# A depthwise convolution on VectorE that takes turns with GpSimd's weight splits

## The reference, cut to what matters

```python
hx = modulate(rmsnorm(x, g_mix), sh1, sc1)
px = hx @ w_in                                  # columns: q, k, v, o, gates, then 2 x 1024 for the convolution
u = p[..., :1024] * sigmoid(p[..., 1024:])      # GLU, then per row of 64 tokens:
y = conv(u, conv_w, width 31, centred, per channel) + conv_b
y = silu(layernorm(y, cn_g, cn_b))
x = x + ga1 * (concat([mlstm(px), y]) @ w_out)
x = x + ga2 * peer(...);  return rmsnorm(x, g_final)
```

## Time and profile before

| | |
|---|---|
| median of 3 runs | 3813.11 us (3805.47 to 3814.7) |
| the profiled execution | 3817.3 us, its span 3814.6 us |
| PE busy | 3521.6 us, 92% of the span |
| POOL busy | 2081.3 us, 55% |
| DVE busy | 2068.7 us, 54% |
| ACT busy | 1104.2 us, 29% |
| mean granted clock of TensorE | 0.96 of full speed |

### The profile page before, as it was taken

How to read it: one execution, slowest core, us unless ns; L and a number is a source line. 1 busy time by engine, 2 the same in 40 slices (tenths; PEclk the granted TensorE clock), 3 DMA queues, 4 the chain that set the end, 5 groups by cost and what they waited for, 6 DMA issues and landing times.

```text
span 3814.6 us, 46495 instructions
## 1 busy us (share of the span) xinstructions
PE 3521.6 (92%) x17646; PEld 3010.7 (79%) x17646; DVE 2068.7 (54%) x3619; ACT 1104.2 (29%) x1240; POOL 2081.3 (55%) x940
## 2 busy tenths in 40 slices
PE   5776679999879979999999999999999999999997
PEld 2554457887457768999999999999888888888885
DVE  1335720010361228699367677765366666667669
ACT  3211112112332222323333344333233232233232
POOL 0255653221133354567666655666677777777773
PEclk8798889999989989999999999999999999999998
DMA  9542345222863232477767766777798888888882
GB/s 343 202 144 88 118 145 179 72 77 67 310 226 122 99 113 94 166 273 272 278 249 283 281 252 260 284 285 298 299 367 314 314 308 315 314 315 310 312 316 110
DMA packets 291478, 874.82 MB, mean 229 GB/s; under 512 B 17361, under 2 KB 78081, under 8 KB 237216
## 3 DMA queue, kind: packets, MB, share of 16 engines
q1 hardware_dynamic: 226224, 519.08, 38.7%
q0 software_dynamic: 38704, 281.20, 18.1%
q10 hardware_dynamic: 26432, 73.02, 5.0%
HBM read 803.82 MB, written 69.37 MB: 229 GB/s over the span
## 4 chain that ended last, share of the span: by engine, by line
PE 81%; DVE 6%; DMA 5%; POOL 5%; ACT 2%; issue 1%; ACTq 0%; DVEq 0%; SPq 0%
PE bank L1733 73%; POOL ring_lo L434 4%; PE bank L2012 2%; PE bank L1926 2%; DMA ring<-in_w_in 2%; DMA neurons<-tiny 2%; PE bank L1741 2%; DMA ring<-in_w_mod 1%; PE bank L1905 1%; DVE low L1322 1%; ACT w_hi L427 1%; DVE acc L1621 0%; PE bank L1995 0%; ACTq L718 0%; DVE b L1510 0%
## 5 line engine op out<-in xcount | busy, mean ns | idle before, releaser
L676 POOL TENSOR_TENSOR split<-ring,split 128x1024 fp32r<-128x1024 f32 x544 | 1304.5, 2409 | 693.5 <-ACT split L996 692.5
L1733 PE MATMUL bank<-h_hi,split 128*128 128x384 f32 (+1 forms) x4608 | 1222.1, 342 | 6.6 <-POOL split L676 5.0
L1733 PE MATMUL bank<-split,a_split 128*128 128x512 f32 x4608 | 1052.3, 391 | 17.1 <-DVE acc L1614 8.8
L996 ACT ACTIVATE split<-ring 128x1024 fp32r<-128x1024 f32 x544 | 577.2, 1062 | 1598.1 <-PE bank L1733 1569.2
L1733 PEld LDWEIGHTS bank<-split,a_split 128*128 128x128 f32 x4608 | 867.6, 188 | 201.6 <-DVE acc L1614 6.3
L1733 PEld LDWEIGHTS bank<-h_hi,split 128*128 128x128 f32 x4608 | 838.6, 188 | 27.7 <-POOL split L676 6.0
L1733 PE MATMUL bank<-h_lo,split 128*128 128x384 f32 (+1 forms) x2304 | 784.8, 341 | 0.0
L434 POOL TENSOR_TENSOR ring_lo<-ring,w_hi 128x2048 fp32r<-128x2048 f32 x47 | 330.3, 7031 | 454.9 <-ACT w_hi L427 454.9
L1733 PEld LDWEIGHTS bank<-h_lo,split 128*128 128x128 f32 x2304 | 433.4, 188 | 9.9
L1733 PE MATMUL bank<-hT_hi,w_hi 128*128 128x512 f32 (+1 forms) x768 | 296.6, 386 | 132.7 <-POOL ring_lo L434 124.9
L1614 DVE TENSOR_TENSOR acc<-acc,bank 128x512 f32<-128x512 f32 x360 | 244.6, 683 | 299.9 <-PE bank L1733 287.2
(11 more groups left out here) (265 smaller groups left out, 3624.4 us busy)
## 6 DMA issues: line engine op xcount, KB each, us to landing
ring<-in_u_emb SPq DMA_DIRECT2D x128, 1024.0 KB
ring<-in_v_emb SPq DMA_DIRECT2D x128, 1024.0 KB
ring<-in_w_mod SPq DMA_DIRECT2D x96, 1024.0 KB
ring<-in_w_in SPq DMA_DIRECT2D x48, 1024.0 KB
neurons<-tiny ACTq DMA_DIRECT2D x128, 192.0 KB
gate_table<-b ACTq DMA_DIRECT2D x6, 4096.0 KB, 14.7
weigh<-neurons SPq DMA_DIRECT2D x32, 768.0 KB
weigh<-gate_table SPq DMA_DIRECT2D x32, 768.0 KB
```

The source lines that it names most:

```text
L676: nc.gpsimd.tensor_tensor(split[:, r % 2, 1, at].bitcast(F32R), ring[:, r % 4, :, :].rearrange("p k n -> p (k n)")[:, at], split[:, r % 2, ...
L996: nc.scalar.activation(split[:, q % 2, 0, at].bitcast(F32R), ring[:, q, :, :].rearrange("p k n -> p (k n)")[:, at], ACT.Copy)\
L1733: last = mm(out_, left[a].bitcast(F32R), right[b].bitcast(F32R), start=start and n == 0, stop=stop and n == 2)
```

## The change

VectorE's 248 convolution instructions are written out without loops, and before every ninth of them (for the first 198), later before every fourteenth, VectorE waits for one more weight split: for the steps n = 0, 9, 18, ... it waits for `wsplit_made` = 10 + n/9, that is until the split of tile r = 9, 10, 11, ... is done, and from n = 198 on for r = 31, 32, 33, 34. The work per step is the same.

The padded buffer is filled by pairs of channel tiles. Behind r = 9 GpSimd makes the first four products as before, but waits for its own two products before it reports each pair. Behind r = 17 it makes the other four: two into the half of `u_pad` that the first 62 steps have freed, two into `convT` tiles 6 and 7, which nothing uses yet. Behind r = 24 it copies those two into `u_pad` with two `tensor_copy` instructions. ScalarE now waits for the products (`glu_used`) where it refills `glu`; the store of o uses the buffer of q (`spill_q`), and ScalarE's wait for the whole convolution moves from block 6 to the emptying of the first k block. Three semaphores of the last stage (`x2_back`, `ga2_loaded`, `g_final_loaded`) become one.

```diff
@@ -206,7 +206,6 @@
         u_pad = top[:, 0:4 * UPW].rearrange("p (c r w) -> p c r w", r=ROWS, w=PADW)
         row_buf_b = top[:, 3072:4096].rearrange("p (b n) -> p b n", b=2)
         spill = top[:, 0:3072]
-        spill_o = spill[:, 0:2048].rearrange("p (m t) -> p m t", t=T)
         spill_q = top[:, 8216:10264].rearrange("p (m t) -> p m t", t=T)
         spill_k = spill.rearrange("p (m t) -> p m t", t=L)
         spill_v = spill.rearrange("p (s n) -> p s n", n=NB)
@@ -324,6 +323,7 @@
         set_free = sem("set_free")
         upad_clear = sem("upad_clear")
         glu_done = sem("glu_done")
+        glu_used = sem("glu_used")
         conv_step = sem("conv_step")
         pass_full = sem("pass_full")
         ln_sub = sem("ln_sub")
@@ -399,10 +399,8 @@
         a_split_made = sem("a_split_made")
         sum_free = sem("sum_free")
         sum_full = sem("sum_full")
-        x2_back = sem("x2_back")
-        ga2_loaded = sem("ga2_loaded")
+        last_rows = sem("last_rows")
         x2s_loaded = sem("x2s_loaded")
-        g_final_loaded = sem("g_final_loaded")
         merge_step = sem("merge_step")
         merged = sem("merged")
         s_step = sem("s_step")
@@ -607,22 +605,40 @@
                     pool.wait_ge(whi_made, 1)
                 nc.gpsimd.tensor_tensor(ring_lo[:, 0, at].bitcast(F32R), ring[:, 0, kk, :], weight_slot(0)[:, at],
                                         op=ALU.subtract).then_inc(first_split if kk < QT - 1 else wsplit_made, 1)
+            def glu_product(half, c, dst):
+                nc.gpsimd.tensor_tensor(out=dst, in0=glu[:, 0, c, :].rearrange("p (r w) -> p r w", w=GRID_W),
+                                        in1=glu[:, 1, c, :].rearrange("p (r w) -> p r w", w=GRID_W),
+                                        op=ALU.mult).then_inc(glu_used, 1)
             for r in range(1, WO_R):
                 split_lo(pool, r)
-                if r in (4 * 2 + 1, 4 * 4 + 1):
-
-                    half = (r - 9) // 8
-                    pool.wait_ge(set_free, 2 + 2 * half + 2)
+                if r == 9:
+                    pool.wait_ge(set_free, 4)
                     pool.wait_ge(upad_clear, 1)
-                    if half:
-                        pool.wait_ge(conv_step, 4 * TAPS)
-                    for cc in range(4):
-                        last = nc.gpsimd.tensor_tensor(
-                            out=u_pad[:, cc, :, TAPS // 2:TAPS // 2 + GRID_W],
-                            in0=glu[:, 0, cc, :].rearrange("p (r w) -> p r w", w=GRID_W),
-                            in1=glu[:, 1, cc, :].rearrange("p (r w) -> p r w", w=GRID_W), op=ALU.mult)
-                        if cc % 2:
-                            last.then_inc(glu_done, 1)
+                    for c in range(4):
+                        glu_product(0, c, u_pad[:, c, :, TAPS // 2:TAPS // 2 + GRID_W])
+                        if c % 2:
+                            pool.wait_ge(glu_used, c + 1)
+                            pool.sem_inc(glu_done, 1)
+                if r == 17:
+                    pool.wait_ge(set_free, 6)
+                    pool.wait_ge(conv_step, 2 * TAPS)
+                    for c in range(4):
+                        glu_product(1, c, u_pad[:, c, :, TAPS // 2:TAPS // 2 + GRID_W] if c < 2 else
+                                    convT[:, 4 + c, :].rearrange("p (r w) -> p r w", w=GRID_W))
+                    pool.wait_ge(glu_used, 6)
+                    pool.sem_inc(glu_done, 1)
+                if r == 24:
+                    pool.wait_ge(conv_step, 4 * TAPS)
+                    pool.wait_ge(glu_used, 8)
+                    for c in (2, 3):
+                        last = nc.gpsimd.tensor_copy(u_pad[:, c, :, TAPS // 2:TAPS // 2 + GRID_W],
+                                                     convT[:, 4 + c, :].rearrange("p (r w) -> p r w", w=GRID_W))
+                        last.then_inc(glu_used, 1)
+                    pool.wait_ge(glu_used, 10)
+                    pool.sem_inc(glu_done, 1)
             for h in range(HEADS):
                 pool.wait_ge(s_copied, 6 * (h + 1))
@@ -795,16 +811,14 @@
                 src = bank[:, s:s + 4, :]
                 if j < 4:
                     if j == 2:
-                        act.wait_ge(glu_done, 2)
+                        act.wait_ge(glu_used, 4)
                     nc.scalar.activation(glu[:, j % 2, :, :], src, ACT.Sigmoid if j % 2 else ACT.Copy)\
                         .then_inc(set_free, 1)
                     return
                 if j == 4:
-                    act.wait_ge(glu_done, 4)
-                if j == 6:
-                    act.wait_ge(conv_step, 8 * TAPS)
+                    act.wait_ge(glu_used, 8)
                 spilled(j - 4)
-                buf = spill_q if j < 6 else spill_o
+                buf = spill_q
                 if j < 6:
                     nc.scalar.activation(buf, src, ACT.Copy, scale=HD ** -0.5).then_inc(set_free, 1)
                 else:
@@ -829,6 +843,8 @@
             def empty_kv(n):
                 spilled(4 + n)
+                if n == 0:
+                    act.wait_ge(conv_step, 8 * TAPS)
                 for b in BANK_ORDER:
                     if n >= 2:
                         dst, src = spill_v[:, b, :], bank[:, b, :]
@@ -1126,7 +1142,7 @@
                 if k == 0:
                     store_neurons(NK - 1, 1)
                     for j in range(JD):
-                        act.dma_start(x2_dense[:, j, :], x2_dram[j * P:(j + 1) * P, :]).then_inc(x2_back, 16)
+                        act.dma_start(x2_dense[:, j, :], x2_dram[j * P:(j + 1) * P, :]).then_inc(last_rows, 16)
                 if k == 3:
                     act.wait_ge(rows_used, SLOTS)
                     nc.scalar.activation(nval, nval, ACT.Gelu).then_inc(nval_gelu, 1)
@@ -1134,10 +1150,10 @@
                     act.wait_ge(act_made, 1)
                     for b in range(2):
                         act.wait_ge(neuron_stored[b], 16 * (NK // 2))
-                    act.dma_start(g_final_row, g_final[:].partition_broadcast(P)).then_inc(g_final_loaded, 16)
+                    act.dma_start(g_final_row, g_final[:].partition_broadcast(P)).then_inc(last_rows, 16)
                     for i in range(LT):
                         act.dma_start(ga2_part[i], mod_dram[3 * D + i * NB:3 * D + (i + 1) * NB].partition_broadcast(P))\
-                           .then_inc(ga2_loaded, 16)
+                           .then_inc(last_rows, 16)
             with act.Fori(1, GROUPS // 2 - 1) as i:
                 for k in range(8):
                     sweep_unit(i * 8 + k, k % 4)
@@ -1235,24 +1251,29 @@
             rest1(KT - 1)
-            for half in range(2):
-                with dve.Fori(0, 2) as i:
-                    dve.wait_ge(glu_done, i + (2 * half + 1))
-                    for tap in range(TAPS):
-                        for cc in range(2):
-                            n = 2 * tap + cc
-                            y = top[:, bass.ds(i * (2 * T) + (4120 + (4 * half + cc) * T), T)]\
-                                .rearrange("p (r w) -> p r w", w=GRID_W)
-                            u = top[:, bass.ds(i * (2 * UPW) + cc * UPW, UPW)]\
-                                .rearrange("p (r w) -> p r w", w=PADW)[:, :, tap:tap + GRID_W]
-                            w = conv_col[:, bass.ds(i * (2 * TAPS) + (4 * half + cc) * TAPS + tap, 1)]
-                            if tap == 0:
-                                nc.vector.tensor_scalar(y, u, w, chan_col[:, bass.ds(i * 2 + 16 + 4 * half + cc, 1)],
-                                                        ALU.mult, ALU.add).then_inc(conv_step, 1)
-                            else:
-                                dve.wait_ge(conv_step, i * (2 * TAPS) + (4 * TAPS * half + n - 1))
-                                nc.vector.scalar_tensor_tensor(y, u, w, y, ALU.mult, ALU.add)\
-                                    .then_inc(conv_step, 1)
+            def conv_turn(n):
+                if n < 198 and n % 9 == 0:
+                    dve.wait_ge(wsplit_made, 10 + n // 9)
+                if n >= 198 and (n - 198) % 14 == 0:
+                    dve.wait_ge(wsplit_made, 32 + (n - 198) // 14)
+            for pair in range(CTILES // 2):
+                dve.wait_ge(glu_done, pair + 1)
+                for tap in range(TAPS):
+                    for cc in range(2):
+                        n = 2 * TAPS * pair + 2 * tap + cc
+                        f = 2 * pair + cc
+                        conv_turn(n)
+                        y = convT[:, f, :].rearrange("p (r w) -> p r w", w=GRID_W)
+                        u = u_pad[:, f % 4, :, tap:tap + GRID_W]
+                        w = conv_col[:, f * TAPS + tap:f * TAPS + tap + 1]
+                        if tap == 0:
+                            nc.vector.tensor_scalar(y, u, w, chan_col[:, 16 + f:17 + f], ALU.mult, ALU.add)\
+                                .then_inc(conv_step, 1)
+                        else:
```

(7 more changed lines are left out.)

## The result

| | before | after |
|---|---|---|
| median | 3813.32 us (4 runs, 3805.47 to 3814.7) | 3692.68 us (4 runs, 3692.18 to 3693.22) |
| profiled execution, its span | 3817.3, 3814.6 us | 3693.22, 3691.2 us |

The ratio is 0.9686 (95% interval 0.9674 to 0.9698). The medians differ by 120.6 us; 113.8 were forecast, and the time of 3692.68 lies inside the range of 3690 to 3713, near its lower end.

What follows compares the result with a forecast made beforehand. TensorE was taken to stall on GpSimd's weight splits, kept out by VectorE's tap runs. A loss of 117.0 us less 1.0, 1.1, 0.9 and 0.2 gave 113.8 off 3813.1: 3699.3 us, range 3690 to 3713.

Steps and rivals of the forecast that it cites:

- What bounded: TensorE waits 114.4 us for GpSimd's weight splits, which runs of back-to-back convolution taps on VectorE keep out whole.
- The loss: Blocks with taps against blocks without, two taking 157.3 against 98.8 us: 117.0 us lost in all.
- The delays: Late splits still expected after the change: 1.0 us from nine-tap groups, 1.1 and 0.9 from buffer refills, 0.2 later.
- the split of r = 18: After GpSimd's second four products, this weight split was expected at +37.4, wanted at +35.2; 1.1 us would stay.
- the two copies: GpSimd's copies into the padded buffer, 1.3 us each, making the split of r = 25 0.9 us late.
- The first k block: A 14-tap group of 9.4 us delays the split of r = 32; cost 0 to 0.7 us, taken as 0.2.
- The sum: Whole execution: 117.0 us less four delays leaves 113.8 us off the front, 3699.3 us from the median.
- Small delays: Rival: semaphore and lock handovers of 1 us each cost 12 to 24 us over six blocks, 3711 to 3723; chance 0.11.
- The ring: Rival: splits and tap groups alternate at 10.7 us, binding from 12.35; slower (3838 us) 0.02, part of its cost (3755) 0.04.
- The signs I named: Splits at most 6 us longer, tap groups about 6 us, TensorE's wait under 15, clock near 1.00, 30 us spare.

## Why the prediction was right, point by point

- *What bounded.* Right. Splits kept out by runs of taps, and nothing else: without the turns the time is back at 3814.3.
- *The loss, 117.0 us.* The runs say 118.7: 413.3 us for six blocks less 6 x 49.1. I had taken a block from the start of one split to that of another whose second, r = 32, belongs to the k block and comes 0.6 us late; measured from place 7 to place 7 two blocks without taps take 98.2, not 98.8.
- *The delays, 3.2 us booked.* This was the mis-sized term. Six blocks take 294.0 us against 294.5 for six without taps, and five blocks of the kernel with the taps left out take 244.8, so 293.8 for six: the delays cost nothing (between -0.5 and 0.2). The step that failed is that a turn must end before the next split can run. It held only for splits that came late in their turn: r = 32 was forecast to be done 14.0 us behind the start of place 7, and was at 13.8. Behind r = 17 the split of r = 18 was to be done 2.2 us late at +37.4; it was done at 360.94 = +34.4, 0.8 us before TensorE wanted it, since it got into the turn behind one tap. Behind r = 24 the two copies took 1.64 us in place of 2.6, and the split of 437.86 was let in too. The first k block, booked at 0.2, cost nothing: it starts 15.0 us behind place 7 where it was 15.1.
- *The sum.* 113.8 + 1.7 + 3.7 = 119.2, and 0.4 us by which this execution was ahead at the start make the 119.7 at the k block. The medians have 120.6. From the k block to the end the profiled executions of all twelve kernels here take 3152 to 3161 us, whatever was changed in front, so the 124.1 between the two profiled executions has 3.7 of that scatter in it. Another 0.7 lies outside the spans: an execution takes 2.5 to 2.7 us more than its span with the kernel before, 2.0 to 2.1 with the changed one. That is most of the 0.9 us by which the medians exceed 119.7; no run shows what it comes from.
- *The rule of the Trainium skill that I set against the trace* ("SBUF — State Buffer", "Who interferes with whom": the lock is held for one instruction, whoever issues first has it). I said that the trace contradicts it. It does for a run of overlapping taps (a split waited 33.75 us), and agrees for a split that comes early in a run (0.5 us for that of 290.22) and for taps with an opening every eighth: no split held longer than 5.13 - 4.6 = 0.5 us.
- *The rivals.* Small delays: not there. The ring as the bound: real, but only with turns of 18 (3766 us); its cost at turns of 9 was nothing, as forecast, since a round of 10.7 us is under TensorE's 12.3; besides, splits get into turns.
- *The signs I named.* The wait of TensorE (7.9 us, under 15), the clock (1.00), the stretched splits (at most 8.85 us) and the last tap (568.77, 36.7 us before TensorE asks at 605.46) came as forecast. But I had also called groups of VectorE longer than 7 us a sign of being wrong, and seven of them are: 16.0 to 26.3 us, two or three turns with one or two splits let in between. The time was right all the same; the picture of turns and splits strictly one after the other was not.
- *What it missed.* The turns are one way to make openings, not the only one: one number in the kernel before gives 99 of the 121 us. The forecast came out right from a cause that it described too coarsely: a run of taps keeps GpSimd out, but not one that GpSimd meets in its first six taps.

## What to carry to other kernels

Where GpSimd's instructions are many times their usual length, look for a run of overlapping VectorE instructions over them, and open it: let every eighth instruction wait until the one before it is complete (0.17 us of idle each time in a loop, 0.04 written out), before building a schedule of turns. Then look at what GpSimd itself waits for, since the spread-out work ends later; the kernel that refills a buffer in smaller parts was another 20 us faster here, and 18 us of waiting for that refill were gone.

## What the runs showed of the hardware

A run of VectorE instructions that overlap head to tail keeps GpSimd out as long as it lasts, if GpSimd's instruction comes more than some 4.2 us (six taps of 0.66) after the run began; before that it is let in behind one instruction. The border is not sharp: splits were let in up to 4.6 us and held from 4.26. Time may not be what counts: in the kernel with `tensor_scalar` taps a split that came 3.5 us into a run, but in its eighth tap (0.46 us apart), was held and took 29.3 us. That is one case.

The exclusion holds for `scalar_tensor_tensor` with two inputs in SBUF and for `tensor_scalar` with one. Two things end it: an instruction that waits for the one directly before it (even 0.04 us of idle is enough), and the change from `scalar_tensor_tensor` to `tensor_scalar` (seven of seven). Why the first six differ, and why the change of instruction lets GpSimd in, is open.

A waiting VectorE instruction does get in between two GpSimd instructions, one at a time: before, the two tap-0 instructions took 9.41 us together beside two splits.
